# Modulation segment 2 multiplied by VectorE in input passes 1 and 2, TensorE summing over partitions, and back transposes at units 4 and 7 of pass 4

## The chip, the cores and the metric

One core of a Trainium2 chip. The metric is the device time of one execution in microseconds. The kernel is written against the engines directly: five programs (TensorE or PE, VectorE or DVE, ScalarE or ACT, GpSimd or POOL, SyncE or SP) run side by side and wait for each other by semaphores. All data is float32.

## The reference

One layer of a diffusion step for 128 prompt tokens and 128 sample tokens (two groups, g = 0 and 1), D = 2048:

```python
mod = (cond @ w_mod + b_mod)[:, None, :]
sh1, sc1, g1, sh2, sc2, g2 = jnp.split(mod, 6, axis=-1)
m, s_f, s_b = _mixer(x * (1 + sc1) + sh1, s0_f, s0_b, *mixer_w)
x = _layernorm(DEEPNORM_ALPHA * x + g1 * m, ln1_g, ln1_b)
f = _moe(x * (1 + sc2) + sh2, *moe_w)
x = _layernorm(DEEPNORM_ALPHA * x + g2 * f, ln2_g, ln2_b)
```

`cond` is one vector for each group, so each of the six segments of the modulation is a product of a 2 x 2048 matrix with a 2048 x 2048 block of `w_mod`. The mixer is one wide projection `h @ w_in` (gated linear attention and a depthwise convolution of 31 taps, each with its part of the columns) followed by `w_out`; `_moe` is a mixture of 16 experts. Segment 2 is `g1`, which scales the output of the mixer.

## The kernel before

**Weights.** SP loads all weights in tiles of 128 x 2048 (units) into a ring of 8 slots, `ring`. Unit n goes to slot n % 8 and waits until unit n - 8 is used: PE counts `used` up behind the last matmul of each unit (`unit`, `segment`, `wide_pass` of the sync block). A segment of the modulation has 16 units (SEG_UNITS), an input pass 8 (PASS_UNITS).

**Order of the units.** Segments 0 and 1 (`first_mod`) are mixed with pass 0. Then come passes 1 to 4 of `w_in`, 1024 columns each. Behind each wide unit of a pass stands one unit of a segment: segment 2 in passes 1 and 2, segment 3 in passes 3 and 4. Then segment 4 in five parts between the steps of the attention, the two passes of `w_out`, segment 5, the experts.

**PE in a pass** (`wide_pass`, line 670). A wide unit is 8 matmuls (two k tiles, four banks of 128 x 512); in the trace each float32 matmul has two records, so it shows as x16, and a segment unit of 4 matmuls as x8. The four banks of pass p are `pass_bank(p, i)`, (4p + i) % 7. The function `after(u)` follows each wide unit: it multiplies the segment's unit (`seg_units`, line 629: the condition vectors, 128 x 32 with two columns filled, against 4 x 512 columns, each on a strip of 32 output rows of bank 7), and at certain units it adds other work: the gate matmuls (line 713), the transposes of u (line 723) after unit 1 of pass 2, and the back transposes of the convolution (line 768) after units 1 and 4 of pass 4.

**Segments 2 and 3 to SBUF.** ACT copies bank 7 to `segrow` (line 459) and POOL adds it to `modrow` (line 360). Segment 4 is added by DVE.

**DVE.** After the columns for h (line 1102) it waits for the end of pass 1, makes u (line 1111), waits for the transposes, copies u (line 1115), and runs the convolution: 8 chunks of channels x 31 taps, one instruction of 128x256 each (lines 1125 and 1129), two chunks interleaved so that no instruction waits for the one just before. Then, for each group, statistics of the transposed result (lines 1138, 1139) and the normalizing (line 1143).

**ACT around pass 4.** Its program has the two Sqrt for the convolution's normalizing (line 469), then the evacuation of pass 4 with Silu (`evac(4, ...)`, line 433), then `segment_out(3)`, then the exponentials of the decays (line 495):

```python
            for g in range(G):
                act.wait_ge(back_var, g + 1)
                nc.scalar.activation(small[:, 32 + g:33 + g], small[:, 51 + 2 * g:52 + 2 * g], ACT.Sqrt,
                                     bias=small[:, 63:64]).then_inc(back_sd, 1)
            evac(4, rs, ACT.Silu)
            segment_out(3)
```

**PE behind pass 4** (`decays`, lines 790 to 797) waits for the evacuated pass and for `seg_out`.

## Time and profile before

| | us |
|---|---|
| median of 3 runs | 1720.81 (1720.03 to 1722.47) |
| profiled execution | 1719.95 |
| its span | 1718.1 |
| PE busy | 1433.8 (83%) |
| DVE busy | 443.7 (26%) |
| ACT busy | 127.1 (7%) |
| mean rate of the DMA engines | 340 GB/s |

The span is that of the instructions in the profile; the execution's own time lies 1.85 us above it. Times in rows are microseconds from the span's start, `mean ns` is the mean of one instruction. Matmuls overlap at their ends, so a group's duration is a little longer than the distance to the next. PEclk is the clock that TensorE was granted, as a part of the full one.

### The profile page before, as it was taken

Reading aid. Unit: us, or ns where it says so; the run is one execution under the profiler, and the core shown is the slowest. Engines: PE = TensorE matmul, PEld = TensorE weight load, DVE = VectorE, ACT = ScalarE, POOL = GpSimd, SP = SyncE. Lnnn points to the kernel's source line nnn. Section 1 sums busy time; section 2 is a strip of 40 time slices with the busy share of each in tenths; the row PEclk is TensorE's granted clock in tenths of the full one; section 3 lists DMA queues with packets and bytes.
Section 4 is the critical chain, followed back from the end, with each engine's and each line's share of the span. In section 5 each row is a group of like instructions: output and inputs, shape, how many; then the busy total and the mean of one; then the engine's idle time right before and its main releaser. Section 6 shows DMA issues by size and latency. Waiting matters only on the chain.

```text
span 1718.1 us, 17166 instructions
## 1 busy us (share of the span) xinstructions
PE 1433.8 (83%) x6847; PEld 621.6 (36%) x6848; DVE 443.7 (26%) x874; ACT 127.1 (7%) x199; POOL 48.5 (3%) x23
## 2 busy tenths in 40 slices
PE   2889999999879996569867768997999966899973
PEld 0434343334444453124313313431445421445422
DVE  0210029920230243311312112222202312201315
ACT  0001200200410000000100000000000000000000
POOL 1000000100000002400000000000000000000000
PEclk8899999999969997679979879998899978899977
DMA  9995666676846188999999999999996999997894
GB/s 352 373 397 193 239 250 247 250 272 255 329 181 235 68 298 356 401 411 417 418 414 416 419 416 415 417 418 413 417 419 242 392 417 413 417 418 282 349 414 170
DMA packets 139461, 584.98 MB, mean 340 GB/s; under 512 B 13491, under 2 KB 15627, under 8 KB 112796
## 3 DMA queue, kind: packets, MB, share of 16 engines
q1 hardware_dynamic: 129408, 562.07, 83.1%
q10 hardware_dynamic: 10012, 22.37, 3.5%
q8 instruction: 25, 0.41, 0.1%
q14 instruction: 16, 0.13, 0.0%
HBM read 581.19 MB, written 3.21 MB: 340 GB/s over the span
## 4 chain that ended last, share of the span: by engine, by line
PE 55%; DMA 38%; DVE 3%; issue 2%; SPq 2%; ACT 1%; DVEq 0%; POOL 0%; ACTq 0%
PE bank L670 20%; DMA late<-in_w_e_down_dram 13%; DMA ring<-in_w_e_up_dram 12%; PE bank L965 12%; DMA ring<-in_w_e_gate_dram 9%; PE bank L978 6%; PE bank L942 4%; PE bank L906 3%; PE bank L629 3%; DMA ring<-in_w_in_dram 2%; DMA ring<-in_w_mod_dram 1%; SPq L280 1%; DMA late<-in_w_e_up_dram 1%; PE bank L1039 1%; PE bank L805 1%
## 5 line engine op out<-in xcount | busy, mean ns | idle before, releaser
L965 PE MATMUL bank<-ring,work 128*32 128x512 f32 (+2 forms) x1536 | 324.0, 708 | 106.7 <-DMA ring<-in_w_e_up_dram 43.5
L670 PE MATMUL bank<-ring,hT 128*128 128x512 f32 x768 | 344.8, 605 | 7.6 <-DMA ring<-in_w_in_dram 4.7
L670 PEld LDWEIGHTS bank<-ring,hT 128*128 128x128 f32 x768 | 145.1, 193 | 203.7 <-issue 199.6
L965 PEld LDWEIGHTS bank<-ring,work 128*32 128x32 f32 (+2 forms) x1536 | 84.2, 133 | 327.8 <-issue 166.1
L942 PEld LDWEIGHTS bank<-work,arena 128*128 128x128 f32 x1088 | 136.9, 208 | 23.7 <-issue 19.2
L942 PE MATMUL bank<-work,arena 128*128 128x128 f32 x1088 | 141.7, 293 | 4.4 <-DVE work L1355 4.4
L1129 DVE SCALAR_TENSOR_TENSOR arena<-work,late,arena 128x256 f32<-128x256 f32 x240 | 95.3, 477 | 0.0
L978 PE MATMUL bank<-ring,work 128*32 128x512 f32 (+2 forms) x512 | 89.1, 595 | 0.0
L965 PE MATMUL bank<-late,work 128*32 128x512 f32 (+2 forms) x256 | 58.2, 762 | 21.1 <-DMA late<-in_w_e_gate_dram 11.7
L965 PE MATMUL bank<-hT,work 128*32 128x512 f32 (+2 forms) x256 | 57.9, 759 | 21.4 <-DMA hT<-in_w_e_gate_dram 10.8
L1367 DVE COPY work<-bank 128x512 f32<-128x512 f32 x68 | 47.0, 691 | 83.6 <-PE bank L942 83.6
L1402 DVE COPY work<-bank 128x512 f32<-128x512 f32 x11 | 7.6, 692 | 229.1 <-PE bank L965 229.1
L978 PE MATMUL bank<-late,work 128*32 128x512 f32 (+2 forms) x256 | 50.8, 641 | 18.0 <-DMA late<-in_w_e_down_dram 18.0
L629 PE MATMUL bank<-ring,late 128*32 128x512 f32 x512 | 65.1, 615 | 0.0
L1380 DVE TENSOR_TENSOR xres<-bank,xres 128x512 f32<-128x512 f32 x88 | 53.6, 682 | 12.0 <-PE bank L1005 12.0
L906 PE MATMUL bank<-ring,hT 128*128 128x512 f32 x128 | 55.3, 592 | 0.0
L643 PE MATMUL bank<-ring,late 128*32 128x512 f32 x256 | 35.5, 680 | 16.6 <-DMA ring<-in_w_mod_dram 16.5
L978 PE MATMUL bank<-hT,work 128*32 128x512 f32 (+2 forms) x256 | 46.4, 593 | 0.6 <-DMA hT<-in_w_e_down_dram 0.6
L978 PEld LDWEIGHTS bank<-ring,work 128*32 128x32 f32 (+2 forms) x512 | 28.9, 125 | 47.8 <-issue 46.1
L1005 PE MATMUL bank<-arena,work 32*128 32x512 f32 x176 | 36.5, 836 | 9.7 <-DVE arena L1412 9.7
L1412 DVE TENSOR_TENSOR arena<-bank,const 128x512 f32<-128x512 f32 x22 | 14.2, 686 | 95.7 <-PE bank L978 95.7
L572 ACT COPY work<-bank 128x512 f32<-128x512 f32 x11 | 6.4, 586 | 436.1 <-PE bank L965 436.1
(233 smaller groups left out, 800.3 us busy)
## 6 DMA issues: line engine op xcount, KB each, us to landing
ring<-in_w_mod_dram SPq DMA_DIRECT2D x96, 1024.0 KB, 7.1
ring<-in_w_e_gate_dram SPq DMA_DIRECT2D x96, 1024.0 KB, 18.6
ring<-in_w_e_up_dram SPq DMA_DIRECT2D x96, 1024.0 KB, 18.6
ring<-in_w_e_down_dram SPq DMA_DIRECT2D x64, 1024.0 KB, 19.0
ring<-in_w_in_dram SPq DMA_DIRECT2D x40, 1024.0 KB, 5.0
hT<-in_w_e_down_dram SPq DMA_DIRECT2D x32, 1024.0 KB, 21.6
late<-in_w_e_down_dram SPq DMA_DIRECT2D x32, 1024.0 KB, 24.2
ring<-in_w_out_dram SPq DMA_DIRECT2D x16, 1024.0 KB, 7.2
```

The costliest lines, as they stand in the source:

```text
L280: sp.dma_start(dst, src).then_inc(slot[n % SLOTS], 16)
L629: last = mm(ps[bank][seg_slice(q), :], condT[:, kt, :], ring[:, n % SLOTS, q * BANK:(q + 1) * BANK], start=(kt == 0), stop=(kt == KT - 1))
L643: last = mm(ps[4 + s][seg_slice(i), :], condT[:, 4 * u + i, :], ring[:, n % SLOTS, i * BANK:(i + 1) * BANK], start=(u == 0), stop=(u == 3))
L670: last = mm(ps[bank[k]][:, :], hT[:, kt, g * P:(g + 1) * P], ring[:, n % SLOTS, i * 1024 + hf * BANK:i * 1024 + (hf + 1) * BANK], start=(k ...
L906: last = mm(ps[4 + 2 * g + hf][:, :], hT[:, kt, g * P:(g + 1) * P], ring[:, at, i * 1024 + hf * BANK:i * 1024 + (hf + 1) * BANK], start=(k ...
L942: last = mm(ps[4 + kt // 4][:, (kt % 4) * P:(kt % 4 + 1) * P], h2[:, g, kt * P:(kt + 1) * P], sel[:, g, :], start=(g == 0), stop=(g == 1))
L965: last = mm(ps[bank][at:at + rows, :], XT[:, kt, 0:rows], buffer(i % DEEP)[:, k * 1024 + hf * BANK:k * 1024 + (hf + 1) * BANK], start=(i < ...
L978: last = mm(ps[bank][at:at + rows, :], weights(i), buffer((16 + i) % DEEP)[:, q * BANK:(q + 1) * BANK], start=(i == 0), stop=(i == FT - 1))
L1005: mm(ps[j][:, :], wselT[r, g, :], yf[r, g * BANK:(g + 1) * BANK], start=True, stop=True).then_inc(st_cmb, 1)
L1129: last = v.scalar_tensor_tensor(convacc[:, cc], src, tapT[:, cc, k:k + 1], convacc[:, cc], ALU.mult, ALU.add)
L1367: v.tensor_copy(XT[:, 4 * i:4 * i + 4, :], ps[4 + i][:, :].rearrange("p (k s) -> p k s", k=4)).then_inc(st_xv, 1)
L1380: v.tensor_tensor(xres[:, g, cs], ps[j][:, :], xres[:, g, cs], ALU.add).then_inc(st_add, 1)
```

## The change

1. Segment 2 is no longer multiplied by PE. For each of its 16 tiles DVE multiplies the 128 x 2048 weights with the condition value of each row (a scalar for each partition), once for each group, and adds it to `segacc`, 2 x 2048 columns (`seg_product`: 32 instructions; 8 tiles before the evacuation of pass 1, 2 after it, 6 inside the convolution, one after each 6 instructions).
2. After unit 4 of pass 3 PE sums `segacc` over the partitions with 8 matmuls into bank 4 (SUM_BANK), the left operand being columns of ones in `rt`. DVE adds the result to `modrow` when 180 of the 248 convolution instructions are issued; the third matmul of pass 4 waits for that (bank 4 is its bank).
3. ACT's copy and POOL's addition for segment 2 go. SP waits for `g1_acc` where a slot held a tile of segment 2, and for `used` elsewhere; `used` no longer counts these 16 units (PE_UNITS, `pass_end`).
4. The back transposes of pass 4 move from units 1 and 4 to units 4 and 7; those of group 1 go to banks 1 and 0. The decays are issued before the wait for the normalized group 1.
5. `grelu` and `attnT`: `grelu` moves to the arena under `rs`, so ACT waits for the gates before it evacuates pass 4; POOL clears `attnT` after the sum instead of at the start.

```diff
 U_BANKS = (5, 6, 0, 5)
-BACK_BANKS = ((6, 0), (1, 6))
+BACK_BANKS = ((6, 0), (1, 0))
+SUM_BANK = 4
 H2T_BANKS = (0, 1, 2, 5)
 STEP_UNITS = 24
 PRE_UNITS = 6 * SEG_UNITS + (PASSES_IN + 2) * PASS_UNITS
+PE_UNITS = PRE_UNITS - SEG_UNITS
 MAX_EXTRA = G * P * 2 // (CAP + 1)
...
         modpart = part(work, 0, 2, BANK)
-        grelu = part(work, 0, 2, BANK)
+        grelu = part(arena, 4096, 2, BANK)
+        segacc = part(work, 0, G, D)
         segrow = part(work, 3072, BANK)
...
 
-            return 2 * SEG_UNITS + PASS_UNITS + 2 * PASS_UNITS * p - (1 if p else 0)
+            return 2 * SEG_UNITS + PASS_UNITS * (1 + p) + max(0, PASS_UNITS * (p - 2) - 1)
 
...
 
-            def unit(dst, src):
+            by_pe, by_dve = [], []
+
+            def unit(dst, src, dve_unit=False):
                 nonlocal n
                 if n >= SLOTS:
-                    sp.wait_ge(used, n - SLOTS + 1)
+                    if n - SLOTS in by_dve:
+                        sp.wait_ge(g1_acc, G * (by_dve.index(n - SLOTS) + 1))
+                    else:
+                        sp.wait_ge(used, by_pe.index(n - SLOTS) + 1)
+                (by_dve if dve_unit else by_pe).append(n)
                 sp.dma_start(dst, src).then_inc(slot[n % SLOTS], 16)
                 n += 1
 
             def segment(s, kts=range(KT)):
                 for kt in kts:
-                    unit(ring[:, n % SLOTS, :], wmod2[kt * P:(kt + 1) * P, s * D:(s + 1) * D])
+                    unit(ring[:, n % SLOTS, :], wmod2[kt * P:(kt + 1) * P, s * D:(s + 1) * D], s == 2)
 
...
         def _(pool):
-            for t in (condT[:, :, :], modrow[:, :, :], lnrow[:, :, :], wgu, attnT, uT):
+            for t in (condT[:, :, :], modrow[:, :, :], lnrow[:, :, :], wgu, uT):
                 nc.gpsimd.memset(t, 0.0).then_inc(s_zero, 1)
...
             def add_segment(s):
-                pool.wait_ge(seg_out, s - 1)
+                pool.wait_ge(seg_out, 1)
                 nc.gpsimd.tensor_tensor(modrow[:, s - 2, :], modrow[:, s - 2, :], segrow, ALU.add).then_inc(seg_add, 1)
 
             gates(1)
             pool.wait_ge(s_bmod, 32)
-            add_segment(2)
             gates(0)
+            pool.wait_ge(g1_ps, 1)
+            nc.gpsimd.memset(attnT, 0.0).then_inc(s_zero, 1)
             add_segment(3)
...
                 act.wait_ge(used, pass_end(2 * s - 2) + 1)
-                if s == 3:
-                    act.wait_ge(seg_add, 1)
                 nc.scalar.copy(segrow, ps[7][:, :]).then_inc(seg_out, 1)
 
             gates(1, GATE_BANKS[1])
             evac(2, qk, ACT.Copy)
-            segment_out(2)
             gates(0, GATE_BANKS[0])
...
                                      bias=small[:, 63:64]).then_inc(back_sd, 1)
+            act.wait_ge(gate_rdy, 4)
             evac(4, rs, ACT.Silu)
...
 
-            act.wait_ge(seg_add, 1)
+            act.wait_ge(g1_add, 1)
             keep(0, g1_row)
...
                         pe.wait_ge(gate_out, 8)
+                    if p == 4 and k == 2:
+                        pe.wait_ge(g1_add, 1)
                     if k == 3:
                         pe.wait_ge(ev[p - 1], 1)
 
                 def after(u):
 
                     s = 2 + (p - 1) // 2
-                    if u == 0 and p == 1:
+                    if u == 0 and p == 3:
                         pe.wait_ge(tap_rdy, 2)
-                    if u == 0 and p == 3:
-                        pe.wait_ge(seg_out, 1)
-                    seg_units(7, [8 * ((p - 1) % 2) + u])
+                    if p >= 3:
+                        seg_units(7, [8 * (p - 3) + u])
+                    else:
+                        skip_unit()
+                    if p == 3 and u == 4:
+                        pe.wait_ge(g1_acc, G * SEG_UNITS)
+                        pe.wait_ge(col_one, 1)
+                        for g in range(G):
+                            for q in range(NQ):
+                                last = mm(ps[SUM_BANK][seg_slice(q), :], rt[:, g, :], segacc[:, g, q * BANK:(q + 1) * BANK],
+                                          start=(g == 0), stop=(g == 1))
+                        last.then_inc(g1_ps, 1)
                     if p == 1 and u == 2:
...
                         u_transposed()
-                    if p == 4 and u in (1, 4):
-
-                        g = (u - 1) // 3
+                    if p == 4 and u in (4, 7):
+
+                        g = (u - 4) // 3
                         if g == 0:
...
                     pe.wait_ge(ev[4], 4)
-                    pe.wait_ge(seg_out, 2)
+                    pe.wait_ge(seg_out, 1)
                 else:
...
 
+            decays(0, 1)
             pe.wait_ge(back_ev, 2)
-            decays(0, 1)
             conv_transposed(0)
...
 
+            link(v.memset(rt[:, 0:2, :], 0.0))
+            link(v.memset(rt[:, 0, 0:1], 1.0))
+            v.memset(rt[:, 1, 1:2], 1.0).then_inc(col_one, 1)
+
+            made = 0
+
+            def seg_product(kt):
+                nonlocal made
+                unit = 2 * SEG_UNITS + PASS_UNITS + 2 * kt + 1
+                dve.wait_ge(slot[unit % SLOTS], 16 * (unit // SLOTS + 1))
+                w = ring[:, unit % SLOTS, :]
+                for g in range(G):
+                    if kt == 0:
+                        last = v.tensor_scalar(segacc[:, g, :], w, condT[:, kt, g:g + 1], None, ALU.mult)
+                    else:
+                        dve.wait_ge(g1_acc, made - 1)
+                        last = v.scalar_tensor_tensor(segacc[:, g, :], w, condT[:, kt, g:g + 1], segacc[:, g, :],
+                                                      ALU.mult, ALU.add)
+                    last.then_inc(g1_acc, 1)
+                    made += 1
+
+            for kt in range(8):
+                seg_product(kt)
             dve.wait_ge(used, pass_end(1))
...
                 v.tensor_tensor(uu[:, g, cs], ps[pass_bank(1, i)][:, :], sig[:, g, cs], ALU.mult).then_inc(ev[1], 1)
+            seg_product(8)
+            seg_product(9)
             for i in range(4):
...
                         done += 1
+                        if done % 6 == 0 and done <= 36:
+                            seg_product(9 + done // 6)
+                        if done == 180:
+                            dve.wait_ge(s_bmod, 32)
+                            dve.wait_ge(g1_ps, 1)
+                            v.tensor_tensor(modrow[:, 0, :], ps[SUM_BANK][:, :], modrow[:, 0, :], ALU.add).then_inc(g1_add, 1)
 
```

On PE, at the end of pass 2 and the start of pass 3. L670 (L683 in the changed kernel) are the matmuls of the wide units, L629 (L638) those of a segment unit. Before:

```order
L629 MATMUL bank<-ring,late 32x512 [waits slot5]
L629 MATMUL bank<-ring,late 32x512 x3
L670 MATMUL bank<-ring,hT 128x512 [waits slot6]
L670 MATMUL bank<-ring,hT 128x512 x7
L629 MATMUL bank<-ring,late 32x512 [waits slot7]
L629 MATMUL bank<-ring,late 32x512 x3
L670 MATMUL bank<-ring,hT 128x512 [waits uT_evacuated,pass1_evacuated,slot0]
```

Of the change:

```order
L683 MATMUL bank<-ring,hT 128x512 [waits slot4]
L683 MATMUL bank<-ring,hT 128x512 x7
L683 MATMUL bank<-ring,hT 128x512 [waits slot6]
L683 MATMUL bank<-ring,hT 128x512 x7
L683 MATMUL bank<-ring,hT 128x512 [waits uT_evacuated,pass1_evacuated,slot0]
L683 MATMUL bank<-ring,hT 128x512 x2
L683 MATMUL bank<-ring,hT 128x512 [waits pass2_evacuated]
```

The segment units between the wide units are gone, and with them the one between the two passes.

On PE, from the last wide unit of pass 4 to the attention. L768 (L792) are the back transposes, L790 (L814) the first matmuls of the decays, L846 (L870) the first transposes of the normalized convolution. Before:

```order
L670 MATMUL bank<-ring,hT 128x512 [waits slot6]
L670 MATMUL bank<-ring,hT 128x512 x7
L629 MATMUL bank<-ring,late 32x512 [waits slot7]
L629 MATMUL bank<-ring,late 32x512 x3
L790 MATMUL bank<-const,arena 128x128 [waits pass4_evacuated,seg_out,gate_ready,conv_normed]
L790 MATMUL bank<-const,arena 128x128 x7
```

Of the change:

```order
L683 MATMUL bank<-ring,hT 128x512 [waits slot6]
L683 MATMUL bank<-ring,hT 128x512 x7
L638 MATMUL bank<-ring,late 32x512 [waits slot7]
L638 MATMUL bank<-ring,late 32x512 x3
L792 MATMUL bank<-const,arena 128x128 [waits conv_normed]
L792 MATMUL bank<-const,arena 128x128 x7
L814 MATMUL bank<-const,arena 128x128 [waits seg_out,pass4_evacuated,gate_ready]
```

The back transposes of group 1 stand between the last unit of the pass and the decays; their wait is for the normalized group 0.

On DVE, in and behind the evacuation of pass 1. L1111 (L1158) makes u, L1115 (L1164) copies its transposes, L1125 and L1129 (L1174 and L1178) are the convolution, L1145 the products of segment 2. Before:

```order
L1111 TENSOR_TENSOR arena<-bank,work 128x512 [waits pass0_evacuated] x3
L1115 COPY work<-bank 128x4x128 [waits uT_ps] x4
L1125 TENSOR_SCALAR arena<-work,late 128x256 [waits uT_evacuated]
L1125 TENSOR_SCALAR arena<-work,late 128x256
L1129 SCALAR_TENSOR_TENSOR arena<-work,late,arena 128x256 [waits conv_chain] x60
```

Of the change:

```order
L1158 TENSOR_TENSOR arena<-bank,work 128x512 [waits pass0_evacuated] x3
L1145 SCALAR_TENSOR_TENSOR work<-ring,late,work 128x2048 [waits g1_products,slot1]
L1145 SCALAR_TENSOR_TENSOR work<-ring,late,work 128x2048 [waits g1_products]
L1145 SCALAR_TENSOR_TENSOR work<-ring,late,work 128x2048 [waits g1_products,slot3]
L1145 SCALAR_TENSOR_TENSOR work<-ring,late,work 128x2048 [waits g1_products]
L1164 COPY work<-bank 128x4x128 [waits uT_ps] x4
L1174 TENSOR_SCALAR arena<-work,late 128x256 [waits uT_evacuated]
L1174 TENSOR_SCALAR arena<-work,late 128x256
L1178 SCALAR_TENSOR_TENSOR arena<-work,late,arena 128x256 [waits conv_chain] x4
L1145 SCALAR_TENSOR_TENSOR work<-ring,late,work 128x2048 [waits g1_products,slot5]
L1145 SCALAR_TENSOR_TENSOR work<-ring,late,work 128x2048 [waits g1_products]
L1178 SCALAR_TENSOR_TENSOR arena<-work,late,arena 128x256 [waits conv_chain] x6
```

Two tiles stand before the u copies, and from there on one tile (two products) after each six convolution instructions.

## Rows read from the trace of the kernel before

**Rows 1.** The page, part 1: busy us, share of the span, instructions.

```profile
PE 1433.8 (83%) x6847; PEld 621.6 (36%) x6848; DVE 443.7 (26%) x874; ACT 127.1 (7%) x199; POOL 48.5 (3%) x23
```

**Rows 2.** Busy time by stretch, passes 1 and 3: PE, PEld, DVE, ACT, POOL, PEclk, DMA.

```profile
168.00:232.00 64.00, 63.89 (x186) 24.95 (x185) 0.00 (x0) 10.25 (x13) 2.53 (x2) 1.00 0.63 231
...
299.00:365.00 66.00, 66.00 (x197) 25.63 (x196) 54.55 (x132) 12.44 (x17) 8.48 (x3) 1.00 0.68 255
```

**Rows 3.** The chain of waits in pass 1: start, us, what.

```profile
175.58 7.06 PE bank L670 x16
182.64 1.00 PE bank L629 x8
```

**Rows 4.** DVE's timeline, passes 1 to 4: start, us, engine, line, operation.

```profile
232.76 2.48 DVE L1111 TENSOR_TENSOR arena<-bank,work 128x512 f32<-128x512 f32 x4 [90.08 <-PE bank L670]
250.46 2.49 DVE L1115 COPY work<-bank 128x512 f32<-128x512 f32 x4 [15.22 <-PE bank L723]
...
253.63 23.84 DVE L1129 SCALAR_TENSOR_TENSOR arena<-work,late,arena 128x256 f32<-128x256 f32 x60
...
329.73 23.83 DVE L1129 SCALAR_TENSOR_TENSOR arena<-work,late,arena 128x256 f32<-128x256 f32 x60
...
408.42 1.43 DVE L1138 BATCH_NORM_STATS2 stats<-bank 128x6 f32<-128x512 f32 x2 [21.24 <-PE bank L768]
409.88 0.21 DVE L1139 BATCH_NORM_AGGREGATE small<-stats 128x2 f32<-128x12 f32 x1
```

**Rows 5.** Groups of DVE by shape: count, busy us, mean ns, idle before.

```profile
L1129 DVE SCALAR_TENSOR_TENSOR arena<-work,late,arena 128x256 f32<-128x256 f32 x240 | 95.3, 477 | 0.0
...
L1250 DVE SCALAR_TENSOR_TENSOR arena<-xres,small,work 128x2048 f32<-128x2048 f32 x2 | 4.7, 2352 | 0.1
```

**Rows 6.** PE's timeline, pass 4 and the attention behind it.

```profile
366.15 7.13 PE L670 MATMUL bank<-ring,hT 128*128 128x512 f32 x16
...
407.29 1.09 PE L768 MATMUL bank<-const,arena 128*128 128x128 f32 x8
...
431.30 1.07 PE L629 MATMUL bank<-ring,late 128*32 128x512 f32 x8
434.09 2.02 PE L790 MATMUL bank<-const,arena 128*128 128x128 f32 x16 [1.73 <-ACT work L459]
...
468.24 2.05 PE L790 MATMUL bank<-const,arena 128*128 128x128 f32 x16 [1.95 <-DVE arena L1191]
...
481.75 3.78 PE L814 MATMUL bank<-work 128*128 128x128 f32 x16 [5.29 <-DVE work L1163]
...
510.15 3.68 PE L872 MATMUL bank<-const,arena 128*128 128x128 f32 x16 [4.66 <-DVE arena L1191]
```

**Rows 7.** ACT's timeline from the second Sqrt to the decays.

```profile
410.13 0.29 ACT L469 ACTIVATE small<-small 128x1 f32<-128x1 f32 x1 [24.71 <-DVE small L1139]
410.44 1.28 ACT L433 ACT_TABLE_LOAD   x1
431.40 1.57 ACT L433 ACTIVATE arena<-bank 128x512 f32<-128x512 f32 x3 [19.68 <-PE bank L670]
...
435.37 1.28 ACT L495 ACT_TABLE_LOAD   x1 [1.42 <-POOL late L360]
436.66 0.60 ACT L495 ACTIVATE work<-bank 128x512 f32<-128x512 f32 x1
```

**Rows 8.** Busy time by stretch in and behind the attention, columns as in rows 2.

```profile
434.00:476.50 42.50, 38.97 (x280) 20.94 (x280) 10.88 (x25) 19.44 (x41) 1.27 (x1) 1.00 0.88 344
481.70:500.60 18.90, 18.18 (x57) 13.50 (x58) 4.85 (x10) 2.25 (x4) 0.00 (x0) 0.50 0.28 114
510.10:514.00 3.90, 3.68 (x16) 3.28 (x16) 2.21 (x4) 0.00 (x0) 0.00 (x0) 0.50 0.88 336
514.00:516.00 2.00, 1.39 (x3) 0.68 (x4) 1.93 (x4) 0.00 (x0) 0.00 (x0) 0.94 0.97 406
```

**Rows 9.** Waits of SP's DMA queue: for whom, us in total, times, longest.

```profile
SPq L334 <- PE bank L629: 31.5, 6, 22.5
```

33 lines of the change are left out of this document (19 added, 14 removed).

## Prediction

> **What bounds the kernel now.** I read the page first, then the busy time by stretch, then the chain of waits inside the passes, then the timelines of DVE, PE and ACT around pass 4. The page shows PE busy 83% of the span and DVE 26% [rows 1]; the share that counts is that of the input passes. There PE has no hole, 63.89 of 64 us in pass 1 and 66 of 66 in pass 3, at a granted clock of 1.00, while the DMA engines are at 0.63 to 0.68 [rows 2]. So in this stage TensorE is the bound, and time taken off it is time taken off the path. The chain of waits gives the unit prices: a wide unit (16 records of 128x512) 7.06 us, a segment unit (8 records, four column strips at once) 1.00 us [rows 3]. DVE is free for 90.08 us before it evacuates pass 1, and for 15.22 us before the u copies of pass 2; then it runs 248 convolution steps until 353.56 [rows 4]. Behind pass 4 the bound changes: a chain ACT, POOL, ACT runs while PE waits 1.73 us and more [rows 6, 7].
>
> **Removed.** Sixteen segment units of passes 1 and 2, 16 x 1.00 = **-16.0 us** [rows 3]. Their weights are still loaded, so the ring must now bring in 7.06 us what it brought in 8.06: from the 255 GB/s of pass 3 [rows 2] that is 291, and the stage behind pass 4 moves 344 [rows 8]. I charge nothing for it; the cover is the lead of four unit pairs in the ring, 28 us. Two boundaries, pass 1 to 2 and 2 to 3, lose the segment unit that stood between the last wide unit and the next pass. There the fourth matmul of the new pass needs the first evacuated bank: three matmuls give 3 x 0.44 = 1.3 us of cover, an evacuation takes 0.6 to 0.7 us (2.48 for four on DVE [rows 4]). Nothing again; without that cover it would be 0.7 us each.
>
> **Added on PE.** The sum over partitions: 8 matmuls of 32x512, the form and strips of two segment units, **+2.0 us** [rows 3]. It waits for all 32 products.
>
> **Added on DVE.** 32 operations of 128x2048. The nearest rows take 2352 ns each, and as the 128x256 form has a mean of 477 ns but a pitch of 23.84/60 = 397 ns [rows 4, 5], I use 2.27 us each, 4.54 us for a tile, 72.6 us in all. The first 8 tiles stand in the idle stretch of 90 us, needing 36; the last of them is loaded when PE has freed the fourth wide unit of pass 1, some 30 us before the stretch ends. Tiles 8 and 9 stand in the 15.22 us, now 13.2 (two segment units less), needing 9.1, so about 4 us remain before PE would wait for the u copies. Tiles 10 to 15 stand in the convolution, one per 6 steps: 4.54 + 6 x 0.40 = 6.9 us, under the 7.06 us of a wide unit, so the ring slots come free as fast as PE frees its own. The convolution starts 10 us earlier and is 27.2 us longer. The g1 addition sits 62 steps before its end: 353.56 - 24.6 - 10 + 27.2 + 0.7 = 346.9. PE's third matmul of pass 4 waits for it; pass 4 started at 366.15 [rows 6], now 366.15 - 16 + 2 = 352.2, with two matmuls 353.0. Slack 6 us, so nothing on the path. Back transposes of group 0 now come after unit 4: the convolution ends at 370.8, unit 4 at about 391. Nothing either. POOL's memset of attnT moves from the head into the convolution; its reader comes 80 us later. POOL's addition for g1 goes, the one for sh2 stays.
>
> **Moved.** The back transposes of group 1 (8 transposes, 1.09 us with the overlap at their end, 1.0 net [rows 6]) leave pass 4 and stand behind its last unit, where PE waited anyhow: **-1.0 us**. But ACT's program still has the two Sqrt ahead of the evacuation of pass 4. Before, the second Sqrt was done at 410.42 and its Silu table at 411.72, 20 us early [rows 7]. Now the order is: last wide unit, its segment unit (0.94 us until the transposes begin), transposes, two BATCH_NORM_STATS2, the aggregate, Sqrt. From the start of the transposes at 407.29 to the end of Sqrt at 410.42 it takes 3.13 us [rows 4, 6, 7]. Then the table load for Silu, 1.28, in the open. So the first Silu starts 0.94 + 3.13 + 1.30 = 5.4 us after the last wide unit, against 0.04 us before [rows 7]: **+5.3 us**. Behind it hangs everything: four Silu, the copy of segrow, POOL's addition, the Exp table load, the decays on PE. DVE's normalizing of group 1 is finished before the decays, so it adds nothing more.
>
> **The clock.** PE now waits 1.73 + 5.3 - 1.0 = 6.0 us before the decays. The rows show both outcomes of a gap: behind one of 1.95 us the decays ran in 2.05 us as behind 1.73 (2.02), so at the full level of 2.4 GHz; behind one of 5.29 us the granted clock was 0.50, the level of 1.2 GHz [rows 6, 8]. Behind one of 4.66 us the transposes at 510.15 ran at 0.50 too, and the 2 us after them have 0.94 [rows 6, 8]. So I expect the decays to begin cold. Their work is of the same dense kind, so I take 4 us cold, half of it lost: **+2.0 us**. Bounds: 0 (it stays full, or ACT's slack hides it) and 9.4 (a cold stretch as from 481.7 to 500.6 us, half lost [rows 8]). I take the price of the transposes because the decays are full-array matmuls and transposes, while that long stretch is mostly 64-row matmuls. The Trainium skill ("TensorE: Matmul & The Clock Gate", section "HAM oscillation — how this bites in real kernels") warns that every burst behind a long wait starts cold again; this speaks against moving the transposes where they lengthen a gap. By that rule the 2.0 us are due, without it the sum would be 2.0 us lower. The rows agree for the gaps of 4.66 and 5.29 us.
>
> The same skill ("ScalarE: Activation LUTs", section "What ACT_TABLE_LOAD costs") adds a drain of 1.38 us to each load of 1.28. By it the sum would be 1.4 us worse; this stands below as rival 2, since the rows don't show it: the load at 410.44 begins 0.02 us after the Sqrt ends [rows 7].
>
> **Sum.** -16.0 + 2.0 - 1.0 + 5.3 + 2.0 = **-7.7 us**. Nothing behind gives it back or holds it: the loads of the experts are released by PE's segment 5 units (waits of up to 22.5 us of the DMA queue on them [rows 9]), so the weight stream starts earlier by the same amount. The profiled execution took 1719.95 us (span 1718.1 and 1.85 around it), so 1712.25; the median of the runs is 0.86 above it, so **1713.1 us**. A measurement of this kernel can tell about 0.2%, 3.4 us, from no change.
>
> **Rivals.**
> (1) The forecast, 1710 to 1716, with the clock falling for some microseconds or not: 63%. Without the fall it is 1711.1.
> (2) The switch from Sqrt to Silu costs ACT more than its load. For: it was never in the open before, the load at 410.44 had 20 us to spare. Against: the load at 435.37 is in the open, and the Exp behind it starts 1.29 us after it began [rows 7]. If ACT lost once more what the load takes, 1.3 us, the time would be 1714.4. 5%, inside the forecast's range. The drain of the Trainium skill's page named above would do this.
> (3) A long cold stretch. The clock falls in the new gap and stays low as from 481.7 on. 18.9 us cold cost 9.4: 1720.5. For: it happened 50 us later in this trace. Against: there it was fed with 64-row matmuls. Between, with 8 to 10 us cold, 1715 to 1716.5. Together 11%, of which 7% within 0.2% of before.
> (4) A gain behind. The cold stretch 481.7 to 500.6 itself depends on where its gap falls; the shift may end it after the 3.78 us of dense matmuls at its head [rows 6], which gives back half of the other 15 us: 1705.6. For: after 510 just such work brought the clock back. Against: it did not here, where the whole stretch has 0.50 [rows 8]. 13%.
> (5) DVE becomes the bound, the slower side. Place: the third matmul of pass 4 waits for the g1 addition, which stands behind the 12 products inside the convolution. Point: beyond the 6 us of slack each us of DVE is lost, so products over 2.27 + 6/12 = 2.8 us begin to cost, and above 3.7 us each the kernel is slower than before by over 0.2% (12 x 1.43 = 17.2, less 6 of slack, less the 7.7 gained). At twice the price, 4.5 us each, it would lose 27.2 - 6 = 21 us against the forecast and end at 1734. For: a POOL or DMA conflict in SBUF could stretch them. Against: the 128x2048 rows have 2.35 us beside loads [rows 5]. 4%.
> (6) The edit does not shorten the passes: the ring starves and PE waits for weights. The 16 us don't come, and what is left is 2.0 - 1.0 + 5.3 + 2.0: 1729. Against: a DMA share of 0.63 to 0.68 [rows 2]. 2%. Mishaps of the same sign at other places have the last 2%, half of them within 0.2%.
>
> **How the numbers follow.** Faster by over 0.2% (below 1717.4): 63 + 5 + 13 + 4 = 85%. Within 0.2%: 7 + 1 = 8%. Slower: 4 + 2 + 1 = 7%. The range of eight in ten takes rivals 1 and 2 (68), about half of rival 4 (7), the short part of rival 3 and its lower edge (5): **1706 to 1718 us**.
>
> **What would show it.** Right: wide units back to back at 7.06 us with no segment units in passes 1 and 2; PE without a hole up to the end of pass 4, which ends 15.0 us earlier (416.4); Sqrt, table load and Silu after it, decays starting 8.1 us behind its last wide unit, at about 0.50 clock; the out projection starting 7 to 8 us earlier. Wrong: a wait of PE on DVE at the third matmul of pass 4 or at the u transposes; waits on the ring in passes 1 to 3; a clock at 1.00 through the decays; or a cold stretch of another length between 465 and 505 us, which would move the total by more than my terms.

## The result, and the profile after

| | before | after |
|---|---|---|
| median of 5 runs | 1720.03 us (1717.39 to 1722.47) | 1703.60 us (1699.89 to 1711.00) |
| ratio | | 0.9911 [0.9883, 0.9938] |
| profiled execution, its span | 1719.95, 1718.1 | 1702.52, 1700.7 |

The change gains 16.4 us, where 7.7 were forecast, and the time lies below the range. The page of the changed kernel, as in [rows 1], with the group of the new products:

```profile
PE 1411.8 (83%) x6735; PEld 614.7 (36%) x6736; DVE 515.0 (30%) x910; ACT 126.6 (7%) x198; POOL 56.3 (3%) x22
...
L1145 DVE SCALAR_TENSOR_TENSOR work<-ring,late,work 128x2048 f32<-128x2048 f32 x30 | 70.0, 2382 | 30.3 <-DMA ring<-in_w_mod_dram 30.3
```

PE is busy for 22 us less and DVE for 71 us more. The chain of waits through passes 1 to 3, against [rows 3]:

```profile
185.44 1.72 PE bank L726 x4
187.16 48.07 PE bank L683 x112
235.22 1.88 PE bank L736 x16
237.10 48.07 PE bank L683 x112
...
285.17 1.00 PE bank L638 x8
286.16 7.06 PE bank L683 x16
```

Wide units now stand back to back. Seven of them take 48.07 us, which is 6.87 each, not the 7.06 that one takes behind a segment unit. The kernel before had wide units of 6.87 us too, behind the gates and behind the transposes; these groups themselves take longer there, behind a segment unit, than above, behind a wide one (L713 against L726 for the gates, L723 against L736 for the transposes). From the chain of waits of the kernel before:

```profile
191.70 1.91 PE bank L713 x4
193.61 6.87 PE bank L670 x16
...
249.84 2.03 PE bank L723 x16
251.86 6.87 PE bank L670 x16
```

PE still has no hole in pass 1, at a clock of 1.00, and DVE, through with the first eight tiles, is idle for 15.48 us before it evacuates the pass (busy time by stretch and DVE's timeline, against [rows 2, 4]):

```profile
168.00:224.00 56.00, 56.00 (x132) 24.80 (x131) 21.95 (x13) 9.89 (x12) 2.71 (x2) 1.00 0.73 267
```

```profile
221.53 2.48 DVE L1158 TENSOR_TENSOR arena<-bank,work 128x512 f32<-128x512 f32 x4 [15.48 <-PE bank L683]
223.93 9.13 DVE L1145 SCALAR_TENSOR_TENSOR work<-ring,late,work 128x2048 f32<-128x2048 f32 x4
...
235.70 2.49 DVE L1164 COPY work<-bank 128x512 f32<-128x512 f32 x4 [2.64 <-PE bank L736]
...
338.12 0.68 DVE L1187 TENSOR_TENSOR late<-bank,late 128x512 f32<-128x512 f32 x1
```

Four products take 9.13 us, 2.28 each, against the 2.27 of the forecast. DVE then still waits 2.64 us for the transposes of u, where about 4 were forecast. Behind pass 4, PE's timeline, against [rows 6]:

```profile
411.25 1.09 PE L792 MATMUL bank<-const,arena 128*128 128x128 f32 x8
...
418.39 3.76 PE L814 MATMUL bank<-const,arena 128*128 128x128 f32 x16 [6.04 <-ACT work L468]
...
467.56 3.50 PE L838 MATMUL bank<-work 128*128 128x128 f32 x16 [5.29 <-DVE work L1218]
...
488.83 3.67 PE L896 MATMUL bank<-const,arena 128*128 128x128 f32 x16 [4.66 <-DVE arena L1247]
```

and ACT's, against [rows 7]:

```profile
414.10 0.29 ACT L477 ACTIVATE small<-small 128x1 f32<-128x1 f32 x1 [24.72 <-DVE small L1194]
414.41 1.28 ACT L444 ACT_TABLE_LOAD   x1
415.70 0.60 ACT L444 ACTIVATE arena<-bank 128x512 f32<-128x512 f32 x1
```

The last wide unit ends at 410.32. Segment unit, transposes, Sqrt, table load and Silu follow in the predicted order, and PE waits 6.04 us before the decays. The granted clock (third value from the right, after the five engines) and what it did here, against [rows 8]:

```profile
418.30:423.00 4.70, 4.61 (x18) 4.12 (x19) 0.34 (x2) 2.37 (x3) 1.26 (x1) 0.52 0.02 3
467.50:470.90 3.40, 3.34 (x16) 3.31 (x16) 0.73 (x2) 0.00 (x0) 0.00 (x0) 0.54 1.03 418
470.90:488.00 17.10, 12.59 (x66) 8.17 (x64) 5.01 (x13) 5.62 (x14) 0.00 (x0) 0.99 0.17 63
493.30:498.00 4.70, 4.70 (x6) 2.12 (x7) 1.91 (x3) 0.00 (x0) 0.00 (x0) 0.51 0.48 197
```

The decays ran at the half level, as predicted. The big difference is in the next two rows: behind the same gap of 5.29 us the second scores were cold for 3.4 us and the clock then came back, where before it stayed at 0.50 for the whole 18.9 us [rows 8]. The last row is the head of the out projection: 4.7 us at half speed, where the kernel before was back at 0.94 ahead of it [rows 8] and at 1.00 in it.

**Ledger.** Intervals between marks on PE's timeline, in us, each read off one trace; the differences add up to that of the spans.

| from, to | before | after | difference | forecast |
|---|---|---|---|---|
| start to the first z matmul | 160.05 | 157.30 | -2.8 | 0 |
| from there to the end of pass 4's last wide unit | 271.31 | 253.02 | -18.3 | -15.0 |
| to the decays | 2.73 | 8.07 | +5.3 | +5.3 |
| to the second transposes of the convolution | 8.49 | 10.00 | +1.5 | +2.0 |
| to the second scores | 39.17 | 39.17 | 0 | 0 |
| to the transposes of y | 28.40 | 21.27 | -7.1 | 0 |
| to the out projection | 4.46 | 4.45 | 0 | 0 |
| out projection to the logits | 111.72 | 114.01 | +2.3 | 0 |
| logits to the end | 1091.7 | 1093.4 | +1.7 | 0 |

The first and the last row are no part of the change: the start of z lies at 155.4 and at 160.1 us in the two traces of the kernel before, and its end part varies by 2.5 us between them. Over all thirteen traces the end part lies between 1088.4 and 1095.7 us, so a time of a single run can't carry a reading of some microseconds; the rows in between can, as the runs below show.

Four things are open: the 3.3 us more in the passes, whether the two clock terms (-7.1 and +2.3) belong to the change or to chance, whether the +5.3 is what the Sqrt costs, and how much slack DVE has.

### The profile page after: what moved, and what is told of

It reads as the page before. It is cut to its first block, busy times and chain, and to the rows that moved or that the text cites. A ratio compares the mean times of both kernels' runs of the same rounds, so it can differ in the third digit from the quotient of the medians.

```text
span 1700.7 us, 16993 instructions
## 1 busy us (share of the span) xinstructions
PE 1411.8 (83%) x6735; PEld 614.7 (36%) x6736; DVE 515.0 (30%) x910; ACT 126.6 (7%) x198; POOL 56.3 (3%) x22
## 4 chain that ended last, share of the span: by engine, by line
PE 55%; DMA 37%; DVE 3%; issue 2%; SPq 2%; ACT 1%; DVEq 0%; ACTq 0%
PE bank L683 20%; DMA late<-in_w_e_down_dram 13%; PE bank L989 12%; DMA ring<-in_w_e_up_dram 11%; DMA ring<-in_w_e_gate_dram 8%; PE bank L1002 6%; PE bank L966 4%; PE bank L930 3%; PE bank L638 2%; DMA ring<-in_w_in_dram 2%; DMA ring<-in_w_mod_dram 1%; SPq L290 1%; DMA late<-in_w_e_up_dram 1%; DMA hT<-in_w_e_gate_dram 1%; PE bank L1063 1%
## 5 line engine op out<-in xcount | busy, mean ns | idle before, releaser
L989 PE MATMUL bank<-ring,work 128*32 128x512 f32 (+2 forms) x1536 | 319.8, 700 | 105.0 <-DMA ring<-in_w_e_up_dram 45.5
L683 PE MATMUL bank<-ring,hT 128*128 128x512 f32 x768 | 343.5, 606 | 7.0 <-DMA ring<-in_w_in_dram 4.2
L683 PEld LDWEIGHTS bank<-ring,hT 128*128 128x128 f32 x768 | 147.2, 194 | 200.3 <-issue 196.0
L966 PE MATMUL bank<-work,arena 128*128 128x128 f32 x1088 | 136.1, 286 | 4.4 <-DVE work L1411 4.4
L966 PEld LDWEIGHTS bank<-work,arena 128*128 128x128 f32 x1088 | 131.3, 201 | 22.0 <-issue 17.5
L1178 DVE SCALAR_TENSOR_TENSOR arena<-work,late,arena 128x256 f32<-128x256 f32 x240 | 95.9, 480 | 0.0
L1002 PE MATMUL bank<-ring,work 128*32 128x512 f32 (+2 forms) x512 | 89.1, 595 | 0.0
L1145 DVE SCALAR_TENSOR_TENSOR work<-ring,late,work 128x2048 f32<-128x2048 f32 x30 | 70.0, 2382 | 30.3 <-DMA ring<-in_w_mod_dram 30.3
L989 PE MATMUL bank<-late,work 128*32 128x512 f32 (+2 forms) x256 | 59.4, 781 | 22.4 <-DMA late<-in_w_e_gate_dram 13.6
L1002 PE MATMUL bank<-late,work 128*32 128x512 f32 (+2 forms) x256 | 53.5, 686 | 23.6 <-DMA late<-in_w_e_down_dram 23.6
L638 PE MATMUL bank<-ring,late 128*32 128x512 f32 x384 | 48.0, 617 | 0.0
L656 PE MATMUL bank<-ring,late 128*32 128x512 f32 x256 | 35.2, 683 | 14.2 <-DMA ring<-in_w_mod_dram 14.2
```

Source lines behind the costliest of these rows:

```text
L638: last = mm(ps[bank][seg_slice(q), :], condT[:, kt, :], ring[:, n % SLOTS, q * BANK:(q + 1) * BANK], start=(kt == 0), stop=(kt == KT - 1))
L656: last = mm(ps[4 + s][seg_slice(i), :], condT[:, 4 * u + i, :], ring[:, n % SLOTS, i * BANK:(i + 1) * BANK], start=(u == 0), stop=(u == 3))
L683: last = mm(ps[bank[k]][:, :], hT[:, kt, g * P:(g + 1) * P], ring[:, n % SLOTS, i * 1024 + hf * BANK:i * 1024 + (hf + 1) * BANK], start=(k ...
L966: last = mm(ps[4 + kt // 4][:, (kt % 4) * P:(kt % 4 + 1) * P], h2[:, g, kt * P:(kt + 1) * P], sel[:, g, :], start=(g == 0), stop=(g == 1))
L989: last = mm(ps[bank][at:at + rows, :], XT[:, kt, 0:rows], buffer(i % DEEP)[:, k * 1024 + hf * BANK:k * 1024 + (hf + 1) * BANK], start=(i < ...
L1002: last = mm(ps[bank][at:at + rows, :], weights(i), buffer((16 + i) % DEEP)[:, q * BANK:(q + 1) * BANK], start=(i == 0), stop=(i == FT - 1))
```

## The experiments

Eleven runs follow: both kernels once more and nine new ones. Ratios are to the kernel before in runs on the same chip (its medians there lay at 1719.1 to 1719.6), with a 95% interval in brackets. "The ledger" is the table above.

### after_again and before_again: both kernels once more

No edit.

> The changed kernel once more, for a second trace. Theory 1 (the part of the gain that I had not forecast is a cold stretch of TensorE between scores and the output of the attention that happened to be short): passes 1 to 3 and the gap before the decays repeat within 0.3 us (last wide unit of pass 4 to the first decays matmul 8.1 us), while the stretch from the second scores matmuls to the transposes of y is either about 21 us, as in the trace of the changed kernel, or about 28 us, as before the change; the time follows it, about 1702 or about 1709. Theory 2 (the change itself shortened that stretch): it is 21 us again and the times stay at 1702 to 1704.

> The kernel before, once more, for a second trace. Theory 1: the stretch from the second scores matmuls to the transposes of y, 28.4 us in the first trace, can be about 21 us here, and then the time is lower by about 7. Theory 2: it is 28 us again.

Measured: after 1702.26 us, 0.9902 [0.9884, 0.9920]; before 1719.63. The ledger of after comes out again within 0.12 us in all rows from the first z matmul to the logits, the short stretch of 21.27 included. Before had its long one again (28.60), and one thing more: the decays of the second head group, which took 2.05 us behind a gap of 1.95 us in [rows 6], here took

```profile
463.59 3.58 PE L790 MATMUL bank<-const,arena 128*128 128x128 f32 x16 [1.95 <-DVE arena L1191]
```

behind the same gap, at a granted clock of 0.55, and the stretch to the second scores 1.6 us more. So a gap of 1.95 us leaves the clock at full in one execution and not in the next: the prediction read a rule into one row. Each kernel repeats its own length of the second scores' stretch in two traces, which speaks for the change's having moved it; early_gate and dve_twice below speak against a fixed link.

### tail_only: only the move of the transposes, in the kernel before

```diff
-BACK_BANKS = ((6, 0), (1, 6))
+BACK_BANKS = ((6, 0), (1, 0))
...
-                    if p == 4 and u in (1, 4):
+                    if p == 4 and u in (4, 7):
...
-                        g = (u - 1) // 3
+                        g = (u - 4) // 3
...
-            pe.wait_ge(back_ev, 2)
             decays(0, 1)
+            pe.wait_ge(back_ev, 2)
```

> The kernel before with one part of the change alone: back transposes at units 4 and 7 of pass 4, group 1 in banks 1 and 0, decays issued before the wait for the normalized group. Theory: the last wide unit of pass 4 ends 1.0 us earlier, and from there to the first decays matmul it takes 8.1 us instead of 2.7 (Sqrt and the Silu table load stand in the open); the decays begin at half clock and lose 1.5 us more; together 5.8 us slower than before, give or take the cold stretch behind the second scores. Rival: the wait is hidden by ACT and POOL anyway, no change within 1 us.

Measured: 1720.03 us over 12 runs, 1.0006 [0.9992, 1.0020]. PE's timeline at the decays, and the busy time by stretch at the second scores:

```profile
432.35 3.75 PE L790 MATMUL bank<-const,arena 128*128 128x128 f32 x16 [6.04 <-ACT work L459]
```

```profile
483.80:503.00 19.20, 18.52 (x57) 13.83 (x58) 4.85 (x10) 2.25 (x4) 0.00 (x0) 0.50 0.24 98
```

The local terms are there: pass 4 is 1.0 us shorter (270.32), the wait before the decays 8.07 instead of 2.73, their clock is at half. That is 6.5 us in the trace, and its execution, 1727.92, was the slowest of the 12. But the median is up only 0.9, with an interval of -1.4 to +3.4, below the 5.8 that were expected. One trace can't say why the other executions were faster; that the clock there gave something back is likely and not shown. A test with the clock held was needed (warm_tail, below).

### early36: the transposes one unit earlier, in the changed kernel

```diff
-                    if p == 4 and u in (4, 7):
+                    if p == 4 and u in (3, 6):
...
-                        g = (u - 4) // 3
+                        g = (u - 3) // 3
```

> The changed kernel with the back transposes at units 3 and 6 of pass 4 instead of 4 and 7. The convolution ends at 365.6 us in the trace of the changed kernel and unit 3 at 377, so nothing waits for it; Sqrt and the table load finish under unit 7. Theory: the transposes of group 1 cost 1.0 us inside the pass again, the gap before the decays is 2.7 us instead of 8.1, the decays begin at full clock: 5.3 + 1.5 - 1.0 = 5.8 us faster than the changed kernel, about 1698 by medians, give or take the cold stretch behind the second scores. Rival: the decays' place is set by POOL or the u path, no gain.

Measured: 1699.45 us, 0.9886 [0.9865, 0.9906]. That is 2.8 us under after_again, but the two intervals overlap; in the traces it is 3.5 us from the first z matmul to the logits. From the last wide unit to the decays it took 4.07 us, not 2.7. ACT's timeline says why:

```profile
406.09 0.29 ACT L477 ACTIVATE small<-small 128x1 f32<-128x1 f32 x1 [24.72 <-DVE small L1194]
...
411.30 1.28 ACT L444 ACT_TABLE_LOAD   x1 [4.91 <-PE bank L683]
412.59 0.60 ACT L444 ACTIVATE arena<-bank 128x512 f32<-128x512 f32 x1
```

The Sqrt was done almost 5 us early, but the table load waited for PE's last wide unit. In the kernel before it had gone directly behind the Sqrt, 20 us ahead of that unit [rows 7]. The difference is a second wait, on `gate_rdy`, between the two in ACT's program. It was not this wait that held: POOL's additions that raise `gate_rdy` had ended at 316.72 us.

### early_gate: that wait moved ahead of the Sqrt

The transposes stay at units 3 and 6, as in early36; on top of that edit:

```diff
+            act.wait_ge(gate_rdy, 4)
             for g in range(G):
                 act.wait_ge(back_var, g + 1)
...
-            act.wait_ge(gate_rdy, 4)
             evac(4, rs, ACT.Silu)
```

> The changed kernel with the back transposes at units 3 and 6 and ACT's wait for the gates ahead of its two Sqrt instead of ahead of the evacuation of pass 4. In the trace with units 3 and 6 the Silu table load stood behind the last wide unit (1.28 us in the open) because the wait for the gates took the load's place in front of it. Theory: last wide unit to decays 2.7 us as before the change instead of 4.1, 1.3 us less and 0.5 to 1.0 less behind it because the gap is shorter: about 1697. Rival: the load has its place for another reason, no change against units 3 and 6 alone (1699.5).

Measured: 1701.00 us, 0.9894 [0.9869, 0.9920]. The stall is gone in the trace, and so is the short stretch (PE's timeline, then busy time by stretch):

```profile
412.01 2.02 PE L814 MATMUL bank<-const,arena 128*128 128x128 f32 x16 [1.73 <-ACT work L468]
```

```profile
459.70:480.20 20.50, 19.82 (x64) 14.43 (x64) 4.85 (x10) 2.25 (x4) 0.00 (x0) 0.53 0.22 89
```

2.72 us to the decays, and these at full clock: both predicted terms removed, 6.9 us, for 0.6 more in the pass. But the stretch of the second scores is back at 28.68, +7.4, and the out projection to the logits at 111.72, -2.3. The median does not show the gain: 1697 was expected, and by the intervals it is not told apart from early36. The six runs lie apart, 1693.79 the lowest, two at 1706 and three within 0.3 us of 1701; that the length of the cold stretch sets this is likely, but only one of them has a trace.

### warm_before and warm_after: the gaps filled

Matmuls whose result nobody reads, in idle banks, stand where PE waits before the second scores (with the wait on `cT_ev` ahead of them) and before the transposes of y; in warm_after also before the decays.

```diff
+            def fill(bank, k):
+                for _ in range(k):
+                    mm(ps[bank][:, :], ident, const[:, 0:BANK], start=True, stop=True)
...
+            fill(6, 5)
             decays(0, 1)
...
             segment_part(4)
+            pe.wait_ge(cT_ev, 16)
+            fill(1, 5)
             scores(1, 0)
...
             outputs(1, 0)
+            fill(1, 4)
```

> The kernel before with idle matmuls of TensorE in two of its gaps: five of 128x512 (ident against the constants, into the free bank 1) ahead of the second scores and four ahead of the transposes of y. Their results are not used. Theory (the granted clock is what made the stretch from the second scores to the transposes of y 28.4 us before and 21.3 after the change): at full clock that stretch is 19.5 us, the transposes of y take 1.9 instead of 3.7, and the time is about 9 to 11 us below the kernel before, 1709. Rival (the stretch is bound by DVE and ACT, not by TensorE's clock): it stays at 28 us, no gain.

> The changed kernel with the same idle matmuls and five more ahead of the decays (into bank 6). Theory: decays to second convolution transposes 8.5 instead of 10.0 us, second scores to transposes of y 19.5 instead of 21.3, transposes of y to out projection 2.6 instead of 4.5, out projection 111.7 instead of 114.0: 7 to 7.5 us below the changed kernel, about 1695. The distance to the kernel before with the same filling, 13 us (18.3 from the passes, minus 5.3 behind them), is then the change's own worth with the clock held; what the two unfilled kernels differ by beyond that is the clock. Rival: the difference stays at 16 to 17 us, so it isn't the clock.

Measured: warm_before 1710.40 us, 0.9939 [0.9920, 0.9958]; warm_after 1695.32, 0.9859 [0.9838, 0.9879]. PE's timeline and the stretch of the second scores in warm_before:

```profile
481.54 2.05 PE L818 MATMUL bank<-work 128*128 128x128 f32 x16 [0.80 <-DVE work L1170]
...
501.36 1.97 PE L879 MATMUL bank<-const,arena 128*128 128x128 f32 x16 [1.03 <-DVE arena L1198]
```

```profile
481.50:501.30 19.80, 18.11 (x88) 11.46 (x88) 6.50 (x15) 5.63 (x14) 0.00 (x0) 1.00 0.37 142
```

No fall of the clock from pass 4 to the out projection, in either trace. The scores take 2.05 us where they took 3.78 [rows 6], the stretch to the transposes of y 19.82 (19.83 in warm_after) where it took 28.40 and 21.27. In warm_after the decays are at full too:

```profile
416.82 2.02 PE L818 MATMUL bank<-const,arena 128*128 128x128 f32 x16 [1.75 <-ACT work L468]
```

What follows: the clock cost the kernel before about 9 us (1719.6 to 1710.4), the changed one about 7 (1702.3 to 1695.3). With the clock held the change is worth 13.0 us in the traces from the first z matmul to the logits (456.2 to 443.3). The medians give 15.1, but the two intervals leave 9 to 18. The unfilled ledger says the same as the filled traces: -18.3 + 5.3 = -13.0 without its clock rows, and these add -3.3 (1.5 - 7.1 + 2.3). So about 13 of the 16.4 us are the change's own work, and the rest is clock.

### warm_tail: tail_only with the gaps filled

```diff
+            fill(6, 5)
             decays(0, 1)
+            pe.wait_ge(back_ev, 2)
```

with the other edits of tail_only and the other two fills.

> The kernel before with the back transposes at units 4 and 7 (as in tail_only) and the idle matmuls in all three gaps: the cost of the move with TensorE's clock held. By medians tail_only had no measurable cost (1720.0 against 1719.1), while its trace had 8.1 us instead of 2.7 from the last wide unit to the decays. Theory (the move costs 5.3 us there and gives 1.0 us in the pass, and tail_only hid that in cold stretches of other lengths): last wide unit to decays 8.1 us, 4.3 us slower than warm_before, about 1714.7 against 1710.4. Rival (the move is free): 1710.

Measured: 1713.57 us over 12 runs, 0.9973 [0.9954, 0.9992], which is 3.2 over warm_before, with intervals that just overlap. In the trace 8.07 instead of 2.73 before the decays and 0.6 less in the pass, 4.8 in all. So the move by itself costs 3 to 5 us. It is the cost of the Sqrt behind the pass: the decays' clock was full here. That the medians of tail_only hid it behind the clock fits this, since here, with the clock held, it shows; what the clock did in tail_only's other runs is on no trace.

### warm_eg: early_gate with the gaps filled

Early_gate's edits and the two fills before the second scores and the transposes of y.

> early_gate with the idle matmuls ahead of the second scores and of the transposes of y: the changed kernel with both of its flaws behind pass 4 mended and the clock held. Theory: from the last wide unit to the decays 2.7 us, no cold stretch from the decays to the out projection (early_gate's trace had 20.5 and 6.5 us of them), against warm_after 5.3 less and 0.9 more in the pass: 4.4 below it, about 1691. Rival (the cold stretches are as frequent as in early_gate): 1697 to 1701.

Measured: 1689.66 us, 0.9826 [0.9801, 0.9851]. That is 5.7 us under warm_after by the medians, where 4.4 were expected, with intervals that overlap. The traces give 4.4 from the first z matmul to the logits: the stall of 5.3 before the decays is gone, and the pass has 0.9 more.

### dve_twice: each product of the convolution stretch made twice

The last 12 products are made a second time into scratch beside; the output doesn't use it.

```diff
+                    if kt >= 10:
+                        if again:
+                            dve.wait_ge(twice, again)
+                        v.scalar_tensor_tensor(part(work, 4096, D), w, condT[:, kt, g:g + 1], w,
+                                               ALU.mult, ALU.add).then_inc(twice, 1)
+                        again += 1
```

> The changed kernel with each of the 12 products inside the convolution made twice on DVE (the second into unused space), to find DVE's slack. In the trace of the changed kernel the g1 addition ended at 338.8 us and the matmul that waits for it was due at 346.9, 8 us of slack. Theory (DVE has 8 us of slack and then counts in full): 12 x 2.27 = 27.2 us more, so TensorE waits 19 us at the third matmul of pass 4 and pass 4 ends 19 us later, 1722. The ring slots are also held longer, so part of the wait may show in pass 3, with the same sum. Rival (the products are hidden altogether): no change.

Measured: 1730.81 us, 1.0071 [1.0046, 1.0097]. PE's timeline:

```profile
310.48 1.07 PE L638 MATMUL bank<-ring,late 128*32 128x512 f32 x8 [1.06 <-DMA ring<-in_w_mod_dram]
...
312.99 7.13 PE L683 MATMUL bank<-ring,hT 128*128 128x512 f32 x16 [1.45 <-DMA ring<-in_w_in_dram]
...
364.36 7.55 PE L683 MATMUL bank<-ring,hT 128*128 128x512 f32 x12 [15.43 <-DVE late L1194]
```

This is rival 5, at the place named: PE's third matmul of pass 4 waits 15.43 us for the g1 addition, and 2.5 us on the ring come before it, 17.9 in all. In after that addition ends at 338.80. Pass 4 starts at 346.0 there, and its first two matmuls (four records) take 1.8, so the third would ask for it at 347.8: 9.0 us of slack. The doubled run agrees: 12 x 2.28 = 27.4 us more on DVE gave 17.9 of waiting, so 9.5 stayed hidden. The passes are 20.2 us longer than in after, 2.2 more than the waits: behind the long one the clock was at 0.50, and twelve records took 7.55 us where 16 take 7.06. Of what the time lies above the expected 1722, 7.4 are the second scores' stretch, which is long again (28.72), less 2.3 in the out projection; the traced run was the fastest of the four, and what the others had beyond it is on no trace.

### all2: warm_eg with segment units of passes 3 and 4 in pairs and the router's gaps filled

If a change between the two kinds of unit costs time of its own, pairs (wide, wide, segment, segment) must save some without removing a matmul. The bookkeeping of passes' ends moves with it, and two more fills stand in the gaps of the router.

```diff
-                        seg_units(7, [8 * (p - 3) + u])
+                        if u % 2:
+                            seg_units(7, [8 * (p - 3) + u - 1, 8 * (p - 3) + u])
```

> warm_eg with the segment units of passes 3 and 4 in pairs (two wide units, then two segment units) and idle matmuls in the two gaps of the routing. Theory on the price of a segment unit (its own 1.00 us and 0.19 us that the next wide unit is longer than one that follows a wide unit, 7.06 against 6.87): 8 changes fewer, so TensorE's time from the z matmuls to the end of pass 4 is 8 x 0.19 = 1.5 us less than in warm_eg (253.6), 252.1. The matmuls in the gaps of the routing let the first gathering begin at full clock, 1 to 2 us. Together about 1688. Rival (the 0.19 us is not a matter of the change between the two forms): 253.6 again.

Measured: 1684.70 us, 0.9801 [0.9774, 0.9827], the fastest of all. PE's timeline in pass 3:

```profile
329.57 14.00 PE L690 MATMUL bank<-ring,hT 128*128 128x512 f32 x32
343.50 1.92 PE L645 MATMUL bank<-ring,late 128*32 128x512 f32 x16
```

By the starts (the next wide unit begins at 345.35), two wide units take 13.93 us and two segment units 1.85, together 15.78 where single ones in turn take 2 x 8.06 = 16.12. From the first z matmul to the end of the last wide unit it is 3.1 us less than in warm_eg (250.61 against 253.73). But not all of this is order: with pairs, two segment units stand behind the last wide unit instead of one, where PE waits for ACT anyhow (2.73 us to the decays in both), so 1.0 us of work has left the interval. The order brings the other 2.1: six wide units at 6.87 instead of 7.06, and seven pairs of segment units at 1.85 instead of 2.00. The 5.0 us between the medians have these 3.1 in them. The router's fills show too: the 64 matmuls of the first gathering take 7.41 us at a clock of 1.00, 10.06 at 0.72 in warm_eg. The intervals of the two runs overlap.

## Why the prediction was wrong in size

**Right: the path.** TensorE bounded the passes, and taking units off it took time off the end: PE without a hole, DMA share up from 0.63 to 0.73 without a wait of PE on the ring, so rival 6 fell. DVE's products cost 2.28 us each, and its slack was 9.0 us, forecast 6: rival 5 is real, but only with the work doubled. The prediction took 0.44 us for a matmul, which is one of its two records; two matmuls are 1.8 us and not 0.8. That made its slack 1 us too small and touched no term of the sum. Warm_after against warm_before gives the change in itself, 13.0 us in the traces.

**Right: the Sqrt behind the pass.** +5.34 us measured, +5.3 forecast, and its parts stand in ACT's rows. Early_gate takes it away entirely, and tail_only and warm_tail show it alone. The Trainium skill ("ScalarE: Activation LUTs", section "What ACT_TABLE_LOAD costs") gives a drain of about 1.38 us on top of each load. The trace does not agree: Silu starts 1.29 us after the load of 1.28 began, and the load 0.02 after the Sqrt ended. Rival 2 fell.

**Wrong: the unit price, "16 x 1.00 = -16.0".** I priced what the segment unit itself takes, not what it does to the group behind it. A wide unit takes 7.06 us behind a segment unit and 6.87 behind another wide one. Fourteen wide units (thirteen of passes 1 and 2 and the first of pass 3) stood behind a removed segment unit, 14 x 0.19 = 2.7 us. The other two removed units stood before the gates of pass 1 and the transposes of u, which became cheaper too, from 1.91 to 1.72 and from 2.03 to 1.88. So each removed unit gave about 1.19. The sum over partitions took 1.72 us on PE, not 2.0. Against that, the moved transposes gave 0.8 and not 1.0, since one wide unit that stood behind transposes now stands behind a segment unit. These are 3.1 of the 3.3 us between -18.3 and -15.0. Most of the rest lies at the head of pass 1, where before and warm_before differ by 0.25 us as well. The kernel before had no two wide units in a row in passes 1 to 4, but it had the price of 6.87 five times, behind the gates and the transposes; the prediction's [rows 3] stop before the first of them. Pairs in all2 confirm it: 2.1 us from order alone.

**Wrong: the clock, "+2.0".** The decays did start cold, at 0.52, for 1.5 us of loss. But the term took the rest of the clock as fixed, and it wasn't: -7.1 at the second scores and +2.3 at the out projection. That is rival 4, which had 13% and a gain of 7.5 on top of the forecast; its picture, the clock coming back behind the dense matmuls at the head of the stretch, is what the rows show. Together with the 3.3 of the unit price it is the whole error: -7.7 - 3.3 - 0.5 - 7.1 + 2.3 = -16.3. That this meets the 16.4 of the medians so closely is luck, as the first and last rows of the ledger move by more. Either error alone would have left the forecast of 1713.1 inside its range, at 1709.8 or 1707.8; it took both to leave it.

**What stays open.** Why the half-speed stretch behind the same 5.29 us gap is long (about 20 us) in before, before_again, tail_only, early_gate and dve_twice, and short (about 3.5) in after, after_again and early36. In the records, read in steps of 0.25 us, the clock fell 0.35 us before the second scores in after and after_again and just at their start in early36, but 1.0 to 1.6 us before them in the five long cases; that goes with the length, but no run set this time on purpose. Early_gate shows that the length is not the change's to keep: with another shift of some microseconds it was long again. The +2.3 of the out projection is its cold head of 4.7 us. It came with every short stretch and is not in four of the long ones, but tail_only has 1.7 of it behind a long one.

## What to carry to other kernels

The price of a unit on TensorE belongs to its neighbours too: read it from rows in the order that the change will make, even if another group stands in the place of the removed one, since what is removed may also remove a change of form. This kernel, with a few waits of 2 to 6 us on TensorE, has a clock term that shifts of some microseconds redrew: measure a change with these gaps filled by idle matmuls, which both separates the terms and, here, gained 7 to 9 us by itself. When work is moved off a full engine to "where it waited anyhow", follow the chain that hangs on it: the 1.0 us of transposes came with 5.3 us of Sqrt and table load.

## What was not expected of the hardware

**A wide unit costs 0.19 us more behind the 32-column strips** (7.06 against 6.87), and so do the gates (1.91 against 1.72); a second segment unit behind a first takes 0.85 instead of 1.00.

**One wait more in ACT's program decides where a table load stands.** With two waits between Sqrt and Silu (`gate_rdy`, long satisfied, and the end of the pass), the load started behind both, after 4.91 us of idle time (early36). With `gate_rdy` ahead of the Sqrt it went at once (404.48, early_gate). But now two waits stand ahead of the first Sqrt, and the Sqrt's own load, at 347.20 in early36, went behind those:

```profile
379.20 1.28 ACT L478 ACT_TABLE_LOAD   x1 [33.95 <-DVE small L1194]
```

There it cost nothing. So in both places one wait let the load go ahead and two did not; which step of the build puts it there, these runs don't show.

**GpSimd is held up by DVE's stream of two-input operations.** POOL's and DVE's timelines of after:

```profile
300.59 16.08 POOL L366 TENSOR_TENSOR arena<-arena 128x512 f32<-128x512 f32 x2 [102.72 <-ACT arena L464]
```

```profile
314.18 2.64 DVE L1174 TENSOR_SCALAR arena<-work,late 128x256 f32<-128x256 f32 x2
```

An addition of that size took 1.26 us elsewhere; here two took 16.08, and ended 2.5 us after DVE's run of convolution steps gave way to one-input operations. Chance made a second case in the kernel before: its addition for segment 2 started at 301.76 us, 0.04 ahead of a pair of DVE's one-input operations, and took 1.26, and the pair took 1.70. In warm_before, the same program up to there, it started 0.04 ahead of the same pair again, but the pair took its usual 0.72 and the addition lost:

```profile
301.57 25.65 POOL L360 TENSOR_TENSOR late<-late,work 128x512 f32<-128x512 f32 x1 [97.61 <-ACT work L459]
```

It ended at 327.22, 1.2 us after DVE's next one-input operation began (326.02), behind 60 two-input ones. Nothing on the path waited in either case, and no run was built to test it, so the link is read from traces. The Trainium skill ("SBUF — State Buffer", section "SBUF: two separate sides") describes an exclusive lock on a port pair between a DVE operation with two SBUF inputs and a GpSimd operation that reads SBUF; the rows agree with it, and show beyond it that a queue of such DVE operations kept the loser out over many of them, not just for one.
